# Recurrent stage of a 26-stage kernel on one NeuronCore: B and K each meet a row of A, R and the identity in one product

## What is computed

```python
def wkv_scan(state0, r, dec, k, v, kk, a, reverse):
    def step(S, inp):
        d_t, k_t, v_t, kk_t, a_t = inp[:5]
        sa = jnp.einsum("bhvk,bhk->bhv", S, -kk_t)
        S = (S * d_t[:, :, None, :] + sa[..., None] * (kk_t * a_t)[:, :, None, :]
             + v_t[..., None] * k_t[:, :, None, :])
        out = jnp.einsum("bhvk,bhk->bhv", S, inp[5]) if emit else None
        return S, out
```

## Time and profile before

| | us |
|---|---|
| runs: median (lowest, highest) | 4497.16 (4488.99, 4500.42), 3 runs |
| the profiled execution: span from first to last instruction | 4494.7 |
| of it the recurrent stage's groups, first product to last output | 2553.1 to 3312.4 |
| groups 1 to 19 roughly, the window 2616 to 3173 (six pairs) | 557 |
| PE busy in the whole span | 3968.2 (88%) |
| DVE, ACT, POOL busy | 1783.3, 901.2, 341.5 |

### The profile page before, as it was taken

The page is one execution under the profiler, slowest core; times in us unless marked ns, Lnnn a source line. Parts: engine busy times, 40 slices in busy tenths (PEclk is TensorE's granted clock), DMA queues, the critical chain, the costliest instruction groups (busy, mean ns, idle before and its releaser), DMA issues. The chain is left out here.

```text
span 4494.7 us, 76284 instructions
## 1 busy us (share of the span) xinstructions
PE 3968.2 (88%) x33912; PEld 2246.1 (50%) x33912; DVE 1783.3 (40%) x2909; ACT 901.2 (20%) x1545; POOL 341.5 (8%) x315
## 2 busy tenths in 40 slices
PE   5999999988999989967999677777778999999986
PEld 2444444434444445534555466676654555554432
DVE  2534444013341028954010144455423454451593
ACT  1410000100000010011001333334312444441101
POOL 0000000000000000000000333222101010000000
PEclk8999999999999989988999599999999999999997
DMA  1133332210332201201222311111101111110220
GB/s 67 48 117 140 131 140 112 103 75 38 149 135 83 82 28 47 63 23 65 95 95 78 141 32 37 42 40 39 73 14 37 64 43 50 54 61 38 65 84 19
DMA packets 74115, 319.87 MB, mean 71 GB/s; under 512 B 7328, under 2 KB 42144, under 8 KB 59488
## 3 DMA queue, kind: packets, MB, share of 16 engines
q1 hardware_dynamic: 65488, 280.86, 17.3%
q0 software_dynamic: 8336, 34.61, 2.2%
HBM read 278.75 MB, written 30.41 MB: 69 GB/s over the span
## 5 line engine op out<-in xcount | busy, mean ns | idle before, releaser
L612 PE MATMUL lin_ps<-hn,ring 128*128 128x512 f32 (+1 forms) x4320 | 1669.7, 545 | 85.6 <-DVE hn L1778 31.8
L612 PEld LDWEIGHTS lin_ps<-hn,ring 128*128 128x128 f32 x4320 | 821.3, 191 | 889.7 <-issue 842.5
L612 PE MATMUL lin_ps<-arena,ring 128*128 128x512 f32 (+3 forms) x2800 | 1140.0, 578 | 38.7 <-DVE arena L2033 24.8
L612 PEld LDWEIGHTS lin_ps<-arena,ring 128*128 128x128 f32 (+2 forms) x2800 | 538.5, 196 | 626.6 <-issue 571.1
L1306 ACT ACTIVATE arena<-lin_ps 128x512 f32<-128x512 f32 (+4 forms) x527 | 312.1, 606 | 1783.9 <-PE lin_ps L612 1783.5
L612 PE MATMUL lin_ps<-arena 64*64 64x64 f32 (+2 forms) x9728 | 467.3, 236 | 108.4 <-issue 48.1
L1778 DVE SCALAR_TENSOR_TENSOR arena<-arena,vec 128x512 f32<-128x512 f32 (+2 forms) x563 | 436.5, 855 | 149.3 <-PE lin_ps L612 148.0
L612 PEld LDWEIGHTS lin_ps<-arena 64*64 64x64 f32 (+1 forms) x9728 | 353.6, 139 | 181.4 <-issue 115.9
L612 PE MATMUL sum_ps<-arena 64*64 64x64 f32 x7136 | 302.2, 223 | 54.0 <-issue 43.5
L612 PEld LDWEIGHTS sum_ps<-arena 64*64 64x64 f32 x7136 | 258.0, 137 | 68.9 <-issue 55.1
L1778 DVE SCALAR_TENSOR_TENSOR arena<-arena,cs 128x512 f32<-128x512 f32 x336 | 230.7, 763 | 0.0
(11 more groups left out here) (174 smaller groups left out, 2838.0 us busy)
## 6 DMA issues: line engine op xcount, KB each, us to landing
arena<-w_mod SPq DMA_DIRECT2D x24, 2048.0 KB, 7.6
ring<-w_up SPq DMA_DIRECT2D x16, 2048.0 KB, 7.6
ring<-w_down SPq DMA_DIRECT2D x16, 2048.0 KB, 7.6
features<-arena POOLq DMA_DIRECT2D x64, 384.0 KB, 2.6
ring<-w_attn SPq DMA_DIRECT2D x16, 1536.0 KB, 6.7
ring<-w_conv_in SPq DMA_DIRECT2D x16, 1024.0 KB, 5.7
ring<-features SPq DMA_DIRECT2D x40, 384.0 KB, 3.5
arena<-features SPq DMA_DIRECT2D x24, 384.0 KB, 3.2
```

What stands on the lines that cost most here:

```text
L612: return pe.matmul(out, lhsT, rhs, start=start, stop=stop)
```

## The change

- B meets a row of three in one product: `moved` is a view of A, identity and R side by side, 3 x 64 columns (for the backward direction read in descending order). `feature_unit` therefore gives q, bt and rb in one matmul of 192 columns, and with K as the stationary side ak, kt and rk.
- The feature buffer is laid out anew to allow it: A0, R0, I, R1, A1, B0, B1, K0, and K1 elsewhere. POOL writes the identity row `fI` once per buffer.
- A feature job covers half a group (4 units, 2 x 384 columns of one PSUM pair). There are five jobs per group: `ends` (qe woven with qt), B twice, K twice, all in the same PSUM pair `gram_ps`; each waits until the one before it has been copied and masked.
- Nothing is woven into `level_z` any more. K's halves follow `chain_u` in levels 1 and 2, `ends` of the next group in level 3, B's halves in level 4 and before `level_fz_ez` of level 5.
- ACT copies nq, btm and ktm by halves, DVE masks rbm, akm and rkm by halves.
- `chain_m` on PE drops the product of identity and state. DVE keeps the decayed state in `sdec` and adds it: two SCALAR_TENSOR_TENSOR of 64 columns and one more multiply in place of one multiply.
- `wg` is one buffer. SP loads the gate row of pair j-1 after the values of pair j+1, and the last one after `y_done` has reached 7; the load of `xs` and the weights for `rw_out` stand behind it.

```diff
+        moved = [[v[:, 0:3, :, :], v[:, 4:1:-1, :, :]] for v in feats]
+        fI = [v[:, 2, :, :] for v in feats]
-        wg, bv = [at(7704, ALL), at(25904, ALL)], [at(8472, ALL), at(25136, ALL)]
+        wg, bv = at(7704, ALL), [at(8472, ALL), at(25136, ALL)]
+        gram_ps = lin_ps[:, 0, :].rearrange("p (c r) -> p c r", c=2)[:, :, 0:6 * CHUNK]
...
-                        if j >= 2:
-                            sp.wait_ge(y_done, j - 1)
-                        sp.dma_start(wg[j % 2], row_of(3, j)).then_inc(gate_in, 16)
                         sp.wait_ge(b_ev, 2 * (j + 1))
                         if j + 1 < KD:
                             sp.dma_start(wv, row_of(2, j + 1)).then_inc(value_in, 16)
+                        if j:
+                            if j > 1:
+                                sp.wait_ge(y_done, j - 1)
+                            sp.dma_start(wg, row_of(3, j - 1)).then_inc(gate_in, 16)
+                    sp.wait_ge(y_done, KD - 1)
+                    sp.dma_start(wg, row_of(3, KD - 1)).then_inc(gate_in, 16)
...
+            def feature_unit(key, G, u):
+                b, i, d = G // 3 % 2, chunk_of(G, u // 2, u % 2), u % 2
+                lhsT = (fK if key else fB)[b][d][:, i, :]
+                to = gram_ps[:, u // 2 % 2, 3 * CHUNK * d:3 * CHUNK * (d + 1)]
+                return heads(to, lhsT, moved[b][d][:, :, i, :])
...
                 for d in range(2):
                     u, i = 2 * c + d, chunk_of(G, c, d)
-                    if pos:
-                        heads(m_ps[:, d, :], turn, mst[pos % 2][:, d, :], True, False)
-                    heads(m_ps[:, d, :], btm[G % 2][:, u, :], ub[:, d, :], pos == 0, False)
+                    heads(m_ps[:, d, :], btm[G % 2][:, u, :], ub[:, d, :], True, False)
                     m = heads(m_ps[:, d, :], ktm[G % 2][:, u, :], vst[j % 2][:, i, :], False, True)
...
+                    o.wait()
+                    for d in range(2):
+                        m = stt(after[:, d, :], m_ps[:, d, :], ends_of(pos)[:, d:d + 1], sdec[:, d, :], ALU.mult, ALU.add)
+                    m.then_inc(m_ready, 1)
+                if pos + 1 < NCH - 1:
+                    dve.wait_ge(m_ready, 11 * j + pos + 1)
+                    o(tt(sdec, after, ends_of(pos + 1).unsqueeze(2).to_broadcast([P, 2, CHUNK]), ALU.mult))
```

More of the change, by code:

```diff
@@ L448, in build, with gram_part, half_group, ends_job @@
         spare_ps = lin_ps[:, 1, 512:1024]
[L450 to L456, removed]
+        def gram_part(n):
+            return gram_ps.rearrange("p c (d n t) -> p c d n t", d=2, n=3)[:, :, :, n, :]
+        def half_group(v, half):
+            return v[:, 4 * half:4 * half + 4, :].rearrange("p (c d) t -> p c d t", d=2)
+        def ends_job(G):
+            return 5 * G + 1
+        def b_job(G, half):
+            return 5 * G + 2 + half
+        def k_job(G, half):
+            return 5 * G + 4 + half
         def chunk_of(G, c, d):
@@ L917, in turn_out, with ends_unit, ready_ends @@
                 m.then_inc(y_mm, 1)
[L919 to L935, removed]
+            def feature_unit(key, G, u):
[3 more added lines that the diff above has]
+                return heads(to, lhsT, moved[b][d][:, :, i, :])
+            def ends_unit(G, u):
+                b, i, d = G // 3 % 2, chunk_of(G, u // 2, u % 2), u % 2
+                crossed(qe_ps[:, u, :], fB[b][d][:, i, :], fA[b][d][:, i, :])
+                return heads(qt_ps[:, u, :], fA[b][d][:, i, :], fB[b][d][:, i, :])
+            def ready_ends(G):
                 if G % 3 == 0:
@@ L1065, in chain_u, with chain_u_features, chain_u_ends @@
                     pe.wait_ge(e_ready, 5 * G + 5)
-                for d in range(2):
-                    m = crossed(u_ps[:, d, :], E_[G % 3][:, 2 * c + d, :], xb[:, d, :])
-                    if name:
-                        product(name, of, d)
-                m.then_inc(u_mm, 1)
-                if name:
-                    for u in range(2, UN):
-                        g = product(name, of, u)
-                    g.then_inc(gram_mm, 1)
+            def chain_u(G, c):
+                await_u(G, c)
+                step_u(G, c, 0)
+                step_u(G, c, 1).then_inc(u_mm, 1)
+            def chain_u_features(G, c, key, of, half):
+                await_u(G, c)
+                step_u(G, c, 0)
+                feature_unit(key, of, 4 * half)
+                step_u(G, c, 1).then_inc(u_mm, 1)
+                features(key, of, half, after=1)
+            def chain_u_ends(G, c, of):
+                await_u(G, c)
+                step_u(G, c, 0)
+                ends_unit(of, 0)
+                step_u(G, c, 1).then_inc(u_mm, 1)
+                ends(of, after=1)
             def chain_m(G, c):
@@ L1112, in _ @@
             bonus_sums(0)
-            ready_q(0)
-            gram("q", 0)
-            gram("qe", 0)
-            ready_qt(0)
-            gram("qt", 0)
+            ready_ends(0)
+            ends(0)
+            for half in range(2):
+                ready_b(0, half)
+                features(0, 0, half)
             for G in range(GROUPS):
@@ L1157, in _ @@
                 level_z(G, 5, also=G)
+                if not last:
+                    ready_b(G + 1, 1)
+                    features(0, G + 1, 1)
                 aside(G, 5)
@@ L1606, in aside @@
                     reset_f(G + 1)
-                if l == 2 and G + 1 < GROUPS:
                     reset_e(G + 1)
@@ L1645, in _ @@
                 values(0, part)
-            take_q(0)
+            for half in range(2):
+                take_b(0, half)
             key_squares(1)
@@ L2243, in _ @@
             start_f(0)
+            for half in range(2):
+                mask_b(0, half)
             for G in range(GROUPS):
@@ L2246, in _ @@
                 for l in range(1, 6):
-                    if l == 1:
-                        masked("ak", G, akm, strict)
-                    if l == 2:
-                        masked("rb", G, rbm, inclusive)
-                    if l == 4 and not last:
-                        start_f(G + 1)
                     if l < 5:
@@ L2257, in _ @@
                     level_e(G, l)
+                    if G and l < 5:
+                        chain_m(G - 1, l - 1)
+                    if l < 3:
+                        mask_k(G, l - 1)
                     if l == 3 and not last:
                         start_e(G + 1)
-                    if l == 4:
-                        masked("rk", G, rkm, inclusive)
-                    if G and l < 5:
-                        chain_m(G - 1, l - 1)
+                        start_f(G + 1)
+                    if l > 3 and not last:
+                        mask_b(G + 1, l - 4)
                     aside(G, l)
```

181 lines of the change are left out of this document (87 added, 94 removed).

## The result

The changed kernel takes **4474.13 us** (median of 6 runs, 4465.12 to 4481.81) where the kernel before, run in turn with it, takes 4498.35 (4488.99 to 4500.64): ratio **0.9948**, 95% interval 0.9934 to 0.9963. That is 24 us less, for the 58 forecast. The sign was right and the size was not: 4474 lies inside the forecast's range, at its slow end, but less than half of the forecast gain is there.

A forecast was written before the change was run, and what follows sets the result against it. The prediction took PE to be held by the arrival of its own instructions, a block per 3.75 us. Terms: groups -63, start +5, end +8, contention -8, sum -58, so 4439 us; range 4390 to 4485.

The forecast's parts named there:

- the forecast's upper end: Recurrent stage: 3.84 us per block of 256 PE instructions; 29 blocks fewer give 111 us, the most possible.
- rival C: Groups: "issue" follows PE's busy time, staying 5.6 us a group; lost overlap of z counts, +47 us, 4544; chance 0.12.
- PE's own work: PE in each group: work grows although instructions fall, +1.75 us per group, 42 us over 24 groups.
- 25.3 us per group, waits on other engines included; with 1.75 it is 27.1: PE's time per group without "issue", before and after; 27.1 in 6.85 blocks is 3.96 us each, over the fetch's 3.75.
- Both engines are half idle ... Cost nothing, by that cover: ACT and DVE in the groups: added copies, masks and state adds cost nothing, the later state being covered by z.
- the 28.3 forecast: Time per group with a fifth of "issue", 1.2 us, left: 2.6 us less, 63 us over 24 groups.
- The lower end of a group: A group at the fetch pace alone, 6.85 x 3.75 = 25.7 us, if other waits fade in the stalls.
- rival A: Groups: the fetch holds everywhere and waits fade in the stalls; a group at 26.2 us, total 4389; chance 0.20.
- Rival B: Groups: hand-overs of the one PSUM pair and DVE's longer chain add 2.5 us per group, total 4500; chance 0.08.
- Start: Start of the recurrent stage: the first z comes later after the first product, at about 2564, +5 us.
- End: End of the stage: rw_out's first weight block arrives late, now issued behind the last gating, +8 us.
- Contention: Near the end of the groups: the 7 MB of loads no longer slow the instruction fetch, -8 us.

The follow-up runs named there:

- 12: Also written asides_three_64: the kernel of asides with each 192-column product as three of 64 columns; ratio 0.9942 to the kernel before.
- asides: Changed kernel with DVE's side work moved to where PE does not wait for it, and ACT's reset of E back in level 2; ratio 0.9805 to the kernel before.
- 3: Changed kernel with each 192-column product as three of 64 columns into the same places; ratio 1.0036 to the kernel before.
- before_again: The kernel before itself, unchanged, run again for its trace on the later chip; ratio 1.0004.
- the early gating: Changed kernel with the gating of the last but one pair of heads earlier in DVE's queue; ratio 0.9926 to the kernel before.

## Why the prediction was wrong

- **The bound was right.** PE waited for its own instructions: 29 packets fewer as counted, and with the side work out of the way the time follows the number of instructions at equal work (12). That it is their arrival, and not their number or their weight loads as such, the traces show: from 2616 to 3120 in the trace of before PE has 93 standstills of over 0.3 us that end in "issue", and all 93 end 1.2 to 1.6 us after a packet of the instruction queue has landed; of the 36 that another engine ended, 3 do. In asides_three_64 it is 80 of 80 and 3 of 31. A block costs 53 / 18 = 2.9 us there, where the forecast's upper end was 3.84. The Trainium skill (Runtime: NRT & Kernel Launch, section Instruction fetch mechanics) would have the fetch hidden; by that, asides_three_64 would be 10 us over asides. It is 0.0137 of the time over it, 62 us: for PE in these groups the measurement decides, and against it. That would have been rival C; "issue" fell by 3.8 us per group, so C is out.
- **PE's own work.** The timeline of PE inside a half of B shows a 192-column record's pace; records come in pairs, one in each row half:

```profile
2702.05 0.32 PE L633 MATMUL lin_ps<-arena 64*64 64x192 f32 x1
...
2702.06 1.30 PE L633 MATMUL lin_ps<-arena 64*64 64x192 f32 x13
```

  That is (1.30 - 0.32) / 6 = 0.163 us, forecast 0.165. Per group busy time grew by 1.2 us as measured and 0.7 at asides' clock, forecast 1.75. Too high; I have not found which term.
- **The step that failed** is "25.3 us per group, waits on other engines included; with 1.75 it is 27.1", with its companion on ACT and DVE, "Both engines are half idle ... Cost nothing, by that cover". The waits were carried over as a constant while the sum was about to put 1.4 us of new DVE work and a second reset on ACT ahead of the side work for which PE waits. The levels' own steps were covered, as stated; the asides weren't looked at. In place of a constant 36.9 us the waits are 71.5: `kk_n` 2.79 us for 1.27 before, `kk_inv` 1.95 for 0.70. The new steps' total was no surprise (DVE +1.9 us per group, forecast up to 2.8; ACT +0.2, forecast 0.6). Their place was, and the bound of a single one: "each new one is between nothing and 0.29", but a quarter of the new multiplies took 0.41 to 1.62 us beside POOL's work. Moving the asides alone took 39 us of waits and 9 us of slow clock from 18 groups and gave 27.6 us a group for the 28.3 forecast.
- **Waits don't fade in stalls.** The lower end of a group and rival A were built on that ("needs other waits to fade in the stalls"). With the stalls put back they kept most of their length (3: 57.3 us for 60.1; 12: 26.2 for 32.2).
- **Rival B** was nearest in time, and wrong in its mechanism: hand-overs of the one PSUM pair (L2134) cost 3.3 us in 18 groups. It had a chance of 0.08, because it was drawn for every level and not for the three places where PE really stood.
- **Half clock** was no term at all. An estimate from PE's busy time, 439.2 us for the 430.0 of asides with the same matmuls, is 9 us in 18 groups.
- **Start:** +5.5, forecast +5 (the stage began 1.6 us earlier; why is open). **End:** PE waited 6.0 us, forecast 8; last u to the end +1.6 to +4.1 in three traces against the first of before (+3.8 to +6.3 against before_again), and 8 us came back with the early gating. **Contention:** forecast -8; the last two groups gave 17.7, of which 5 by the forecast's own rate of 2.6 a group. Some 12 are left, for the 8 forecast: "issue" fell there by 14.1 us, where the steady rate of 3.8 a group would give 7.5, and PE's clock was 0.82 and then 0.93.
- That the total is 24 and not some 12 us below is therefore owed to the last two groups, without side work and with the 7 MB moved away from them.

## What to carry to other kernels

When an edit takes away the stall that paces an engine and gives other engines new steps for it, the other waits of that engine don't stay what they were: list each of them with what is queued ahead of its releaser before and after, the side work above all. It was the new steps ahead of the side work that made the waits long, not the missing stall: with the stalls back they stayed (3). A fixed order on four engines has to be set anew after such a change, and here that was worth more than the change itself. And an added step need not take the time of the one that it replaces where its operands lie elsewhere: look at what runs beside it (here POOL). And the number of TensorE instructions is a price by itself when matmuls are as short as 64 columns.

## What the runs showed of the hardware that I had not expected

- Where PE had done nothing for 2.2 us in the middle of a busy stage, it was granted 1.2 GHz for the next 3.4 us. Not each such standstill has a fall: in each of the three traces of the changed kernel 13 are 2 us or longer, and 8, 5 and 7 have one beside them. With two matmuls of constants in such waits 2 falls were left of 14.
- The count of falls differs from one execution to the next with the waits on ACT and DVE the same (12, 8 and 14), and with it the time, by 7 us.
- Three 64-column matmuls (and three weight loads) for one of 192, everything else equal, cost 59 to 62 us of 4422 over 24 groups.
- PE's standstills without a visible cause ended 1.2 to 1.6 us after an instruction packet had landed, 93 of 93 in one trace.
- A multiply of 128 columns on DVE with both operands in SBUF took 0.29 us, or up to 1.62 when it began inside an operation of POOL, and then ended 0.15 us behind that one.
